# Recurrence of a two-block model: the state chain moves between the products of the next inverse

## The reference

```
def step(state, inp):
    r_t, w_t, k_t, v_t, kk_t, a_t = inp
    sa = jnp.einsum('bhvk,bhk->bhv', state, kk_t)
    state = (state * w_t[:, :, None, :]
             - sa[..., None] * (kk_t * a_t)[:, :, None, :]
             + v_t[..., None] * k_t[:, :, None, :])
    return state, jnp.einsum('bhvk,bhk->bhv', state, r_t)
```

## Time and profile before

| what | us |
|---|---|
| median of 3 runs | 3225.43 (3218.33 to 3232.19) |
| the profiled execution | 3224.59 |
| its span | 3222.8 |
| stage of the four calls, layer 0 | 358.8 to 537.7 |
| stage of the four calls, layer 1 | 1266.1 to 1445.7 |

### The profile page before, as it was taken

One profiled execution on the slowest core, in us unless ns is written; L12 is line 12 of the kernel. 1 busy time (PEld: TensorE's weight loads), 2 busy tenths in 40 slices (PEclk: granted clock), 3 DMA queues, 4 the chain that ended last, 5 costly groups with the idle time before them and its releaser, 6 DMA issues.

```text
span 3222.8 us, 45044 instructions
## 1 busy us (share of the span) xinstructions
PE 2814.8 (87%) x17755; PEld 2256.1 (70%) x17755; DVE 1738.2 (54%) x2009; ACT 1404.0 (44%) x1718; POOL 80.5 (2%) x114
## 2 busy tenths in 40 slices
PE   7998888899999988888999889676988987888888
PEld 5876677777888764777778677454866776766676
DVE  4546535555555556347455554654574664445564
ACT  4443233435444433235344334643663663345463
POOL 0001000000000010000000000000000000011000
PEclk9999898999999998889999899876998998988899
DMA  4558502444544487014344424111343443521343
GB/s 185 188 203 295 217 29 71 148 164 173 195 170 188 176 292 279 2 65 185 135 167 182 170 105 158 61 59 60 131 163 144 156 171 115 182 99 56 122 157 125
DMA packets 74155, 479.15 MB, mean 149 GB/s; under 512 B 8910, under 2 KB 13100, under 8 KB 19856
## 3 DMA queue, kind: packets, MB, share of 16 engines
q1 hardware_dynamic: 60608, 440.43, 36.7%
q0 software_dynamic: 8784, 32.30, 2.8%
q10 hardware_dynamic: 4608, 4.20, 0.5%
HBM read 468.20 MB, written 2.13 MB: 146 GB/s over the span
## 4 chain that ended last, share of the span: by engine, by line
PE 61%; DVE 13%; ACT 7%; issue 6%; DVEq 5%; DMA 5%; ACTq 3%; POOL 0%; SPq 0%; POOLq 0%
PE ACC L388 49%; DVE w_lo L1325 5%; PE M L388 4%; PE TP L388 4%; DMA raw<-wstream 3%; ACT w_hi L909 3%; PE TP L464 2%; ACTq L1250 1%; PE TP L643 1%; DVEq L1899 1%; DVEq L1894 1%; DVE ST L1819 1%; ACT CV L1259 1%; DMA PREV<-V 1%; DVE PR L1835 1%
## 5 line engine op out<-in xcount | busy, mean ns | idle before, releaser
L1325 DVE TENSOR_TENSOR w_lo<-raw,w_hi 128x2048 fp32r<-128x2048 f32 x371 | 839.4, 2290 | 529.2 <-ACT w_hi L909 510.9
L909 ACT ACTIVATE w_hi<-raw 128x2048 fp32r<-128x2048 f32 x371 | 700.7, 1917 | 514.5 <-DMA raw<-wstream 275.5
L388 PE MATMUL ACC<-w_hi,HA_hi 128*128 128x512 f32 x2064 | 823.8, 399 | 64.5 <-DVE w_lo L1325 23.9
L388 PE MATMUL ACC<-w_lo,HA_hi 128*128 128x512 f32 x2064 | 811.9, 393 | 0.0
L388 PE MATMUL ACC<-w_hi,HA_lo 128*128 128x512 f32 x2064 | 811.9, 393 | 0.0
L388 PEld LDWEIGHTS ACC<-w_hi,HA_hi 128*128 128x128 f32 x2064 | 395.9, 192 | 157.3 <-issue 34.4
L388 PEld LDWEIGHTS ACC<-w_hi,HA_lo 128*128 128x128 f32 x2064 | 395.1, 191 | 83.4
L388 PEld LDWEIGHTS ACC<-w_lo,HA_hi 128*128 128x128 f32 x2064 | 396.3, 192 | 78.7
L388 PE MATMUL ACC<-w_hi,FT_hi 128*128 128x512 f32 x616 | 248.0, 403 | 25.3 <-ACTq L1250 19.4
L388 PE MATMUL ACC<-w_lo,FT_hi 128*128 128x512 f32 x616 | 246.4, 400 | 0.0
L388 PE MATMUL ACC<-w_hi,FT_lo 128*128 128x512 f32 x616 | 246.2, 400 | 0.0
(11 more groups left out here) (301 smaller groups left out, 3171.0 us busy)
## 6 DMA issues: line engine op xcount, KB each, us to landing
raw<-wstream SPq DMA_DIRECT2D x371, 1024.0 KB, 4.9
ADW<-wada SPq DMA_DIRECT2D x48, 1024.0 KB, 13.4
BC<-vecs POOLq DMA_DIRECT2D x19, 512.0 KB, 6.3
BIAS<-toe ACTq DMA_DIRECT2D x32, 128.0 KB, 2.8
BC<-mod_scr POOLq DMA_DIRECT2D x6, 512.0 KB, 6.3
PREV<-R POOLq DMA_DIRECT2D x4, 448.0 KB, 7.0
PREV<-K POOLq DMA_DIRECT2D x4, 448.0 KB, 5.6
PREV<-V POOLq DMA_DIRECT2D x4, 448.0 KB, 9.4
```

The lines of the kernel that those rows point to most:

```text
L388: return pe.matmul(*a, skip_group_check=True, **k)
L909: act.activation(w_hi[:, s, :], unit, ACT.Copy).then_inc(sem["hi_ready"], 1)
L1325: dve.tensor_tensor(w_lo[:, s, :], unit, w_hi[:, s, :].bitcast(F32), ALU.subtract).then_inc(sem["lo_ready"], 1)
```

## The change

- `wkv_chain` is cut into `chain_values`, `chain_state`, `chain_solve` and `chain_update`. The pieces of call n-1 run inside call n, for n = 1, 2, 3: values after the second of the four transposes' groups; state of chunk 0 between the gram pairs; solve of chunk 0 behind the second pair; update of chunk 0 in round 1; then state, solve and update of chunk 1 in rounds 2, 3 and 4, each between the two kinds of products of a round. The chain of call 3 runs by itself behind call 3.
- The pieces write the ACC banks (A4) and no longer TP and M. `ABT` and `LG` have two buffers each, and the fifth round's result goes to a buffer of its own, `XF`.
- `mod_chunk` writes M0 instead of an ACC bank and moves from between the gram pairs to the place ahead of round 1; `mod_sums` moves behind round 1 and writes M1; DVE reads each chunk's sums in its own call (`mod_read`) instead of all at the end.
- ACT and DVE follow: ACT copies PM and U of chunk 0 ahead of the first XX copy, and those of chunk 1 ahead of the XX copies of rounds 2 and 3. DVE does its part of the chain behind the masks of rounds 1 and 4.

The core of the diff:

```diff
-        ABT = ar("ABT", 64, [P, 4, 4, P])
-        LG = ar("LG", 72, [P, 8, 256])
+        ABTS = ar("ABT0", 64, [P, 4, 4, P]), ar("ABT1", 56, [P, 4, 4, P])
+        LGS = ar("LG0", 72, [P, 8, 256]), ar("LG1", 80, [P, 8, 256])
+        XF = ar("XF", 54, [P, 8, CHUNK])
...
-                        wkv_parallel(l, g, t)
-                        wkv_chain(g, t)
+                for n in range(4):
+                    wkv_call(l, n)
+                chain_values(3)
+                for ch in range(2):
+                    chain_state(3, ch)
+                    chain_solve(3, ch)
+                    chain_update(3, ch)
...
+                    if n and p == 1:
+                        chain_values(n - 1)
...
-                    if pair == 0:
-                        mod_chunk(l, 8 + 2 * g + t)
-                mod_sums(l, 8 + 2 * g + t)
+                    if n and pair == 0:
+                        chain_state(n - 1, 0)
+                if n:
+                    chain_solve(n - 1, 0)
...
                 pe.wait_ge(sem["lg_ready"], c.next("lg_ready"))
+                mod_chunk(l, 8 + n)
...
                         last.then_inc(sem["t_ready"], 1)
+                    if n and j == 1:
+                        chain_update(n - 1, 0)
+                    if n and j == 2:
+                        chain_state(n - 1, 1)
+                    if n and j == 3:
+                        chain_solve(n - 1, 1)
+                    if n and j == 4:
+                        chain_update(n - 1, 1)
...
+                    if j == 1:
+                        mod_sums(l, 8 + n)
...
+            def chain_update(n, ch):
+
+                g, t, LG, rows = n // 2, n % 2, LGS[n % 2], CHUNKS[ch]
+                pe.wait_ge(sem["u_copied"], c.next("u_copied"))
+                for k in range(8):
+                    p, of = k // 2, CHUNKS[k % 2]
+                    last = mm(A4[2 + ch][of, CHUNK * p:CHUNK * p + CHUNK], AA[rows, t, head(g, k)], U[rows, k, :],
+                              start=False, stop=True)
+                last.then_inc(sem["s_ready"], 1)
...
 # ACT
+                if n:
+                    chain_part(CHUNKS[0])
+                    chain_solved(CHUNKS[0])
...
+                    if n and j == 2:
+                        chain_part(CHUNKS[1])
+                    if n and j == 3:
+                        chain_solved(CHUNKS[1])
...
 # DVE
+                    if n and j in (0, 3):
+                        chain(n - 1, j // 3)
+                    if j == 1:
+                        mod_chunk(l, 8 + n)
```

More of the change, by code:

```diff
@@ L696, in wkv_parallel @@
                         last.then_inc(sem["u_ready"], 1)
+                    if j == 1:
+                        mod_sums(l, 8 + n)
                 pe.wait_ge(sem["x_ready"], c.next("x_ready", 2))
[L699 to L722, removed]
-                        last = mm(TP[ch][of, CHUNK * p:CHUNK * p + CHUNK], AA[rows, t, head(g, n)], U[rows, n, :],
-                                  start=False, stop=True)
-                    last.then_inc(sem["s_ready"], 1)
-                    for n in range(8):
-                        last = mm(M[1][rows, CHUNK * n:CHUNK * n + CHUNK], LG[rows, n, CHUNK:P], U[rows, n, :],
-                                  start=False, stop=True)
-                    last.then_inc(sem["y_ready"], 1)
-                pe.wait_ge(sem["y_done"], c.next("y_done", 2))
-                pe.wait_ge(sem["s_done"], c.next("s_done"))
@@ new lines, in chain_values @@
+            def chain_values(n):
+                g, t, LG = n // 2, n % 2, LGS[n % 2]
+                if n:
+                    pe.wait_ge(sem["y_done"], c.next("y_done", 2))
+                    pe.wait_ge(sem["s_done"], c.next("s_done"))
+                for a in range(2):
+                    for k in range(8):
+                        for tok in CHUNKS:
+                            mm(A4[a][tok, CHUNK * k:CHUNK * k + CHUNK], LG[tok, k, P + CHUNK * a:P + CHUNK * a + CHUNK],
+                               V[tok, t, head(g, k)], start=k == 0, stop=False)
@@ new lines, in chain_state @@
+            def chain_state(n, ch):
+                g, t, ABT, rows = n // 2, n % 2, ABTS[n % 2], CHUNKS[ch]
+                if t == 0 and ch == 0:
+                    pe.wait_ge(sem["s_zero"], c.next("s_zero"))
+                if ch:
+                    pe.wait_ge(sem["s_done"], c.next("s_done"))
+                for p in range(4):
+                    last = mm(A4[0][rows, P * p:P * p + P], ABT[:, p, 0, rows], S[:, p, :], start=False, stop=True)
+                last.then_inc(sem["pp_ready"], 1)
+                for p in range(4):
+                    mm(A4[1][rows, P * p:P * p + P], ABT[:, p, 1, rows], S[:, p, :], start=False, stop=False)
+                for k in range(8):
+                    p, of = k // 2, CHUNKS[k % 2]
+                    mm(A4[2 + ch][of, CHUNK * p:CHUNK * p + CHUNK], K[rows, t, head(g, k)], V[rows, t, head(g, k)],
+                       start=p == 0, stop=False)
@@ L1039, in wkv @@
                         split(1)
[L1040 to L1046 removed]
+                if n == 3:
+                    for rows in CHUNKS:
+                        chain_part(rows)
+                        chain_solved(rows)
             def mixer(l):
```

149 lines of the change are left out of this document (87 added, 62 removed).

## The result

The changed kernel takes 3186.3 us (median of 4 runs, 3174.3 to 3193.2) beside 3222.3 for the kernel before on the same chip: a ratio of 0.988, with a 95% interval of 0.984 to 0.992. The forecast was 3187. The profiled execution took 3190.9 us, of which the span is 3189.1.

The account below looks back on a forecast made before the run. PE, busy 87% of the span, bounds the kernel. Call 0, three merged calls, splits and tail sum to 160.5 us per layer against 179.25; 37.5 off 3224.6 gives 3187 us, own range 3177 to 3197 (chance 0.60).

Parts of the forecast that it names:

- the relay: Chain of a call: PE's groups wait in turn for ACT's and DVE's results, with no other work running through it.
- Price of the pieces and of the rounds: Pieces cost 4.85 us of PE issue per chunk; five rounds with their pieces and the sums take 22.7 us.
- Front: Start of a call up to round 1: 13.1 us at the upper clock, 15.9 at the lower, 14.5 taken.
- relay and clock: The 5.3 us of a call's chain left beside the 9.7 us of PE issue, not divided further.
- Call 0: First call of the stage, without pieces: 29.6 us instead of 29.3, between 27.4 and 31.
- Splits: Calls 2 and 3: DVE's second w_lo delays round 5's first mask, so PE waits 1.5 us; bounds 0 and 2.3.
- Tail: End of the stage behind call 3: values 1.9 us and a chain by itself, 14.4 us.
- One sign of failure: The prediction is wrong if, among other signs, the granted clock of a call is below 0.9.
- Low fronts with a second stretch: Rival: all fronts at the lower clock plus a second low stretch within each call, 3203 us; chance 0.18.
- Issue alone: Rival: pieces fill all PE stops and the clock is high, 3159 to 3177 us, middle 3168; chance 0.12.
- The relay only moves: Rival: late U or masks make PE stand inside the merged calls, up to 5.3 us per call, 3219 us; chance 0.07.
- Slower: Rival: the lower clock holds through the merged calls, 56 us a call against 44.3, 3295 us; chance 0.03.

Follow-up runs that it names:

- e5_double: Changed kernel with each solve's 8 products issued twice, the second over the first; 3207.8 us (one run), no ratio.
- e7_filler: Kernel before, with idle products on constants into an unused ACC bank where PE waits in the chain; 3195.6 us, ratio 0.992.
- e10_after_filler: Changed kernel with 60 idle products ahead of the barrier before the stage and more in call 3's chain; 3173.9 us, ratio 0.984.
- e3_split: Changed kernel with DVE's second w_lo of calls 2 and 3 behind round 5's masks instead of ahead of them; 3187.0 us, ratio 0.989.
- e8_again: Changed kernel run once more, unchanged, in five rounds on the chip of these runs; 3188.6 us, ratio 0.989.
- e11_long: e9_best with 88 idle products ahead of the stage instead of 60; 3155.9 us, ratio 0.979.
- e6_all: Changed kernel with mod_chunk between the XX turns, second w_lo behind round 5's masks, chunk 1's pieces between the halves of TP<-XX,LG; 3170.7 us, ratio 0.982.
- e4_place: Changed kernel with the pieces of rounds 2 to 4 put between the two halves of TP<-XX,LG; 3193.0 us, ratio 0.991.
- e9_best: e6_all plus idle products ahead of the stage (60) and in its tail; 3158.6 us, ratio 0.980.

## Why the prediction was right, and which steps of it were not

The number was right, and so was the mechanism in its main part: the relay's waits vanish under other products, and a piece costs its issue. That the number came within 1 us is in part luck, since errors of both signs cancel in it, and the clock's share of the gain was not seen. Step by step:

**Price of the pieces and of the rounds: right.** The rounds of call 1 took 22.70 us; the forecast had 22.7. The wait for ACT's copy stands where it stood in the earlier trace rows, and is as long:

```profile
422.67 0.68 PE L389 MATMUL TP<-XX,LG 64*64 64x64 f32 x16 [0.22 <-ACT XX L1087]
```

e5_double shows the same from the other side: a piece in a round costs its issue.

**Front: right in its parts, wrong in its clock.** At the upper level I had 13.1 us and call 1 shows 13.45; the second turn of XX waited 1.05 for 0.9. The 16 transposes had been read short by 0.4: from 358.82 to the next group at 362.58 they took 3.76 and not 3.4, so the lower clock's price for them was too small. But I took half of the fronts as slow, 14.5. The fronts of calls 1 and 2 are fast in both layers, with transposes of 272 ns. The lower level came for 3.4 us behind call 2's wait for w_lo, into the front of call 3, and elsewhere at the start of the stage, in call 0 and in the tail. That is why call 1 took 36.15 and not 37.2. All transposes of this shape and operand, ns min, median and max, which answers the earlier trace rows:

```profile
L653 PE MATMUL TP<-K__56,R x32: 272/273/421, 366.4 to 1365.9; 128*128 128x128 f32 x32
```

**The clock as a share of the gain: not seen.** The forecast named the chain's other 5.3 us "relay and clock" and never split them. e7_filler does: of the 8.1 us that an inner call gives, 3.6 are clock and 4.5 relay. For the stage, 24 us less of the lower level at 0.36 is an estimated 8.7 us, half of its 17.6, and a third at the 0.25 of e10_after_filler's layer 0. I had ranked the clock as an uncertainty of 8.4 us for both stages together; it was a third to a half of the gain.

**Call 0: too low by 1 to 2 us.** 29.6 against 31.6 and 30.4. The gram pairs with nothing between them cost the stop of 1.58, which the forecast had between its bounds; the stop of 1.91 ahead of the second XX turn it had at 0.9. In layer 0 the clock is also low behind them and at the start.

**Splits: right in kind and in size.** 1.5 forecast, 1.58 read, with the chain of causes as given: DVE's part of the chain, then w_lo, then the mask of round 5. Call 2 is longer than call 1 by 1.52 us in layer 1, and by 2.09 in layer 0, where the clock fell at its end. But these stops had a second price that the term left out: e3_split gained 6.6 us for waits of 3.2.

**Tail: too low by 1 to 2 us.** 16.3 for values and chain; from chain_values(3) to the end it took 16.9 us in layer 0 (510.5 to 527.4) and 17.8 in layer 1 (1400.4 to 1418.2), with low clock in both. The chain of waits shows the same group of products, values and the first state products, in either layer (start, us, what):

```profile
510.51 5.53 PE ACC L389 x112
...
1400.43 6.25 PE ACC L389 x112
```

**Sum.** 161.5 us for 160.5, mean of the layers. Call 0 is 1.4 above the forecast, call 1 is 1.05 below, call 2 0.75 below (38.24 and 37.67 for 38.7), call 3 up to its values 0.35 above (38.4 and 39.7 for 38.7), and the tail 1.05 above: 1.0 together, the errors of both signs nearly cancelling. One sign of failure that I had named did appear, a call whose granted clock is below 0.9: call 0 of layer 0, at 0.86, and it is a call without pieces. The rest of the span, outside the two stages, changed by 1.5 us, though the first starts 7.3 later, which e8_again does not repeat.

**The rivals.** Low fronts with a second stretch: refuted in calls 1 and 2; the clock fell behind PE's stops (for 3.4 us behind the 1.58 of call 2, and in layer 0 behind the 1.91 of call 0), not at every front. The transposes themselves run at 272 ns in calls 1 and 2, and in e11_long the clock stays at 1.00 through all 16; but these are 2.4 us only, so what a longer row of transposes would do is not shown. Issue alone: the stops stayed, as the handover above shows; e6_all takes some of them and comes to 34.84 for a call, against 33.5 of pure issue in the forecast. That sum took off 2.0 us of waits in the rounds where 0.7 of them had been taken off before; by its own terms it is 34.2, and the rival's lower bound 3163. The relay only moves: in calls without a split it doesn't; with a split, e4_place shows that it can, 1.0 and 1.5 us in call 2. *Slower* is refuted: call 1 takes 36.15 us at a granted clock of 1.00.

## What to carry to other kernels

Where an engine runs a chain of short products with handovers between them, look at the granted clock beside the waits. Here the stop of 1.58 us in call 2 was followed by 3.4 us at 0.50, and an edit that took out 3.2 us of such waits gained 6.6 (e3_split); and idle products into a free bank showed within one run how much of a stage was clock (12.4 us of 179, e7_filler). In this kernel, moving a dependent chain between the products of the next, independent piece of work paid twice for that reason (3.6 us of clock and 4.5 of relay in an inner call), but it needs second buffers, and the pieces should stand where they delay no engine that the next wait hangs on (e4_place: 1.0 and 1.5 us more in call 2). Of a heavy unit on a helper engine (a split of 2.29 us here), ask what small result stands behind it, before asking whether the engine has time.

## What the runs showed of the hardware

- In the kernel before, PE has five stops of 0.48 to 1.25 us in the 15 us of a chain with a call behind it. The clock fell to 0.50 within seven of the eight chains, each time for 3.4 us; in all it was low for 40 us of the 179 of a stage. Products on constants in these stops took that to 5 and 6 us, and the stage from 179.1 to 166.7 (e7_filler). Behind single stops of 1.05 us, in calls 1 and 2 of the kernel after, it did not fall; behind one of 1.93 us it fell in layer 0 of e9_best and not in layer 1.
- In this stage, made of small fp32 products, one us at a granted clock of 0.50 cost an estimated 0.36 us (12.4 us for 34 less in e7_filler, 4.5 for 12.5 in layer 1 of e10_after_filler), and 0.25 in layer 0 of e10_after_filler (1.3 for 5.2).
- The stop at the end of the stage reached into what follows. In the kernel after, PE stopped for 1.54 us at the barrier, and the clock fell 0.8 us behind it, for 3.4 us; in e9_best, with idle products in the tail, the stop was 0.23 us and the clock stayed at 1.00. The us in which it fell, and the first 4 us behind the barrier, in the kernel after and in e9_best, PE alone:

```profile
528.00:529.00 1.00, 1.00 (x4) 0.63 0.40 49
...
527.40:531.40 4.00, 3.97 (x11) 0.61 0.59 183
```

```profile
507.30:511.30 4.00, 4.00 (x18) 1.00 0.66 206
```

  18 products start where 11 did.
- The transposes of R, 128x128 fp32, took 272 ns (273 the median) at 1.00 in the kernel after and 421 at 0.50 in the kernel before. In e11_long 16 of them, 2.4 us, held the upper level in both layers, behind stops of 1.23 and 0.30 us.
